# Norms of a two-block network: sums of squares with the tokens on partitions, the scale brought back by a unit-matrix product, means in column quarters

## The reference, cut to what matters

```python
def layer_norm(x, g, b):
    x32 = x.astype(jnp.float32)
    mu = jnp.mean(x32, axis=-1, keepdims=True)
    var = jnp.mean(jnp.square(x32 - mu), axis=-1, keepdims=True)
    return ((x32 - mu) * lax.rsqrt(var + LN_EPS) * g + b).astype(x.dtype)
...
        h = rmsnorm(x, norm_ffn_g[layer])
        x = x + swiglu_ffn(h, ffn_w_gate[layer], ffn_w_up[layer], ffn_w_down[layer])
    return rmsnorm(x, final_g)
...
        x = layer_norm(alpha * x + g1 * ax, ln1_g[i], ln1_b[i])
        fx = sqrelu_mlp(x * (1.0 + sc2) + sh2, mlp_w1[i], mlp_w2[i])
        x = layer_norm(alpha * x + g2 * fx, ln2_g[i], ln2_b[i])
```

## Time and profile before

| | |
|---|---|
| median of 3 runs | 3063.86 us (3062.43 to 3078.8) |
| the profiled execution | 3063.69 us |
| its span, first to last instruction | 3061.9 us, so 1.8 us lie around it |
| PE busy | 2767.5 us, 90% of the span |
| PEld, DVE, POOL, ACT busy | 71%, 45%, 44%, 23% |
| mean granted TensorE clock | 0.958 of full speed |
| DMA | 236.37 MB, 77 GB/s |

### The profile page before, as it was taken

How to read it: one execution, slowest core, us unless ns; L and a number is a source line. 1 busy time by engine, 2 the same in 40 slices (tenths; PEclk the granted TensorE clock), 3 DMA queues, 4 the chain that set the end, 5 groups by cost and what they waited for, 6 DMA issues and landing times.

```text
span 3061.9 us, 38477 instructions
## 1 busy us (share of the span) xinstructions
PE 2767.5 (90%) x13722; PEld 2174.0 (71%) x13722; DVE 1378.1 (45%) x1901; ACT 695.2 (23%) x1284; POOL 1345.4 (44%) x822
## 2 busy tenths in 40 slices
PE   7599999978999989889989999999778888899997
PEld 5366777756777768555668888888567667678885
DVE  6964222264222254444344433444675555354544
ACT  2022000012000022555321000100355455111102
POOL 6215556544555553122337443343262222486661
PEclk9799999989999999899999999999989998999999
DMA  4014444423444431000011111111101000122321
GB/s 176 28 49 138 150 147 141 148 86 119 144 137 144 143 111 63 21 1 0 14 42 62 55 62 62 61 55 62 35 28 41 27 33 22 58 89 94 96 96 48
DMA packets 66443, 236.37 MB, mean 77 GB/s; under 512 B 7104, under 2 KB 8512, under 8 KB 66112
## 3 DMA queue, kind: packets, MB, share of 16 engines
q1 hardware_dynamic: 65792, 233.64, 23.1%
q10 hardware_dynamic: 576, 1.70, 0.2%
HBM read 233.22 MB, written 2.10 MB: 77 GB/s over the span
## 4 chain that ended last, share of the span: by engine, by line
PE 76%; DVE 12%; issue 7%; ACT 3%; POOL 2%; DVEq 1%; DMA 0%; ACTq 0%; POOLq 0%; SPq 0%
PE ps L458 59%; PE ps L737 3%; PE ps L492 2%; PE ps L839 2%; PE ps L589 1%; PE ps L811 1%; PE ps L723 1%; PE ps L861 1%; DVE X L1664 1%; PE ps L507 1%; DVE rstd L1278 1%; POOL X L435 1%; DVE hlo L1654 1%; DVE arena L1369 1%; PE ps L708 1%
## 5 line engine op out<-in xcount | busy, mean ns | idle before, releaser
L369 POOL TENSOR_SCALAR whi<-raw 128x1024 fp32r<-128x1024 f32 x334 | 374.2, 1120 | 1343.9 <-DMA raw<-in_stream 1343.6
L458 PE MATMUL ps<-Ahi,whi 128*128 128x512 f32 (+1 forms) x2208 | 770.8, 379 | 132.6 <-DVE Alo L1305 41.5
L371 POOL TENSOR_TENSOR wlo<-raw,whi 128x1024 fp32r<-128x1024 f32 x334 | 823.9, 2467 | 27.9
L458 PE MATMUL ps<-Alo,whi 128*128 128x512 f32 (+1 forms) x2208 | 762.3, 375 | 0.0
L458 PE MATMUL ps<-Ahi,wlo 128*128 128x512 f32 (+1 forms) x2208 | 759.3, 374 | 0.0
L458 PEld LDWEIGHTS ps<-Ahi,whi 128*128 128x128 f32 x2208 | 396.4, 193 | 236.5 <-issue 63.9
L458 PEld LDWEIGHTS ps<-Ahi,wlo 128*128 128x128 f32 x2208 | 396.4, 193 | 74.9
L458 PEld LDWEIGHTS ps<-Alo,whi 128*128 128x128 f32 x2208 | 397.3, 193 | 70.4
L458 PE MATMUL ps<-hhi,whi 128*128 128x512 f32 x1120 | 377.0, 374 | 21.5 <-DVE X L1664 21.5
L458 PE MATMUL ps<-hhi,wlo 128*128 128x512 f32 x1120 | 372.8, 370 | 0.0
L458 PE MATMUL ps<-hlo,whi 128*128 128x512 f32 x1120 | 372.5, 370 | 0.0
(11 more groups left out here) (193 smaller groups left out, 2901.6 us busy)
## 6 DMA issues: line engine op xcount, KB each, us to landing
raw<-in_stream SPq DMA_DIRECT2D x430, 512.0 KB, 3.7
X<-in_xT SPq DMA_DIRECT2D x2, 1024.0 KB, 6.4
arena<-in_dft SPq DMA_DIRECT2D x1, 2048.0 KB, 17.3
out_xT<-X SPq DMA_DIRECT2D x2, 1024.0 KB, 4.3
X<-in_ctxT SPq DMA_DIRECT2D x1, 1024.0 KB, 18.5
arena<-in_icnt ACTq DMA_DIRECT2D x1, 1024.0 KB, 6.6
vec<-in_vec SPq DMA_DIRECT2D x1, 364.5 KB, 7.8
arena<-in_fmap SPq DMA_DIRECT2D x1, 256.0 KB, 12.8
```

What stands on the lines that cost most here:

```text
L369: pool.tensor_scalar(whi[:, s, part], raw[:, s, part], 1.0, 1.0, ALU.mult, ALU.mult).then_inc(sem("w_hi"), 1)
L371: pool.tensor_tensor(wlo[:, s, part], raw[:, s, part], whi[:, s, part], ALU.subtract).then_inc(sem("w_split"), 1)
L458: mm = pe.matmul(dst[c], w[:, b % RING, off:off + P], rhs(k, part, c0, n), start=(k == 0 and w is whi and part == 0), stop=(k == kn - 1 an ...
```

## The change

All nine norms take the form of the norm over heads. For each of the 8 tiles PE does 4 products (6 in l1 and l2) with 128x128 squares as stationary operand and one moving column of ones, where it did one or two products with 512 or 256 moving columns. ACT takes the root of 128x4 or 128x6 into the small tile sm, DVE the reciprocal of it (signal `inv`), and PE brings it back with 4 or 6 products against the unit matrix `ident`, 128 columns each, into PSUM (`norm_scale`, signal `rstd`). DVE then reads the scale from PSUM instead of from SBUF. Since POOL cannot read PSUM, DVE copies the scale to rstd at the end of l1, l2 and l3, and POOL waits for this copy (`kept`) where it waited for the last scaled tile (`m`).

The sums for the mean are taken in parts: tiles 0 to 6 by products with 32 columns of ones into one of four quarters of the partitions, tile k into quarter k modulo 4; ACT copies the partial sums times 1/32 to std; then PE adds up tile 7 and the parts with products of the full ones. The unit matrix is loaded as the third transfer of the kernel, ahead of vec and of the first weights, where it stood behind the constants.

```diff
+PARTS = {"l1": 0, "l2": 0, "l3": 0, "l4": 0}
+MEAN = {"l1": 2, "l2": 2, "l3": 1, "l4": 1}
+SQUARES = {"n1": 6, "n2": 0, "n3": 0, "n4": 0, "n5": 0, "l1": 0, "l2": 0, "l3": 2, "l4": 2}
+RSTD = {"n1": 7, "n2": 5, "n3": 7, "n4": 5, "n5": 3, "l1": 4, "l2": 4, "l3": 4, "l4": 3}
+EARLY = KT - 1
...
+        def norm_scale(name, c0, n):
+
+            return psf[:, RSTD[name] * 512 + c0:RSTD[name] * 512 + c0 + n]
+
         def keys(n):
             return [*range(*window(n)), *range(QT, NTT)]
...
                 sp.dma_start(X[:, 4 * h:4 * h + 4, 0:T], ins["xT"][:, 4 * h:4 * h + 4, :]).then_inc(sem(f"x{h}"), 16)
+            sp.dma_start(ident[:, :], ins["ident"]).then_inc(sem("unit"), 16)
             sp.dma_start(vec[:, :], ins["vec"]).then_inc(sem("vec"), 16)
             for b in range(RING):
...
-                pool.wait_ge(*when(f"{name}_m", len(cols) * KT))
+                pool.wait_ge(*when(f"{name}_kept", 1))
...
-            def column_sums(name, bank, cols, src, src_ready):
-
+            def norm_squares(name, cols):
+
+
+                tokens = sum(n for _, n in cols) // P
                 for k in range(KT):
-                    pe.wait_ge(*when(src_ready, k + 1))
-                    for c, (c0, n) in enumerate(cols):
-                        mm = pe.matmul(ps[:, bank + c, 0:n], ones[:, :], src(k)[:, c0:c0 + n],
-                                       start=(k == 0), stop=(k == KT - 1))
-                    mm.then_inc(sem(name), 1)
-
-            def squares(k):
-                return tmp[:, k % 4, :]
-
-            def rms(name, bank=0):
-                column_sums(f"{name}_sum", bank, X_ONLY, squares, f"{name}_sq")
-
-            def layernorm(name, cols, x_ready, x_before, bank=0):
-
-                for k in range(KT):
+                    pe.wait_ge(*when(f"{name}_sq", k + 1))
+                    for t in range(tokens):
+                        mm = pe.matmul(ps[:, SQUARES[name], t:t + 1], tmp[:, k % 4, t * P:(t + 1) * P], ones[:, 0:1],
+                                       start=(k == 0 and t == 0), stop=(k == KT - 1 and t == tokens - 1),
+                                       skip_group_check=True)
+                    mm.then_inc(sem(f"{name}_sum"), 1)
+                pe.wait_ge(*when(f"{name}_inv", 1))
+                for t in range(tokens):
+                    mm = pe.matmul(norm_scale(name, t * P, P), sm[:, 1, t:t + 1].to_broadcast([P, P]), ident[:, :],
+                                   start=True, stop=True, skip_group_check=True)
+                mm.then_inc(sem(f"{name}_rstd"), 1)
+
+            def layernorm(name, cols, x_ready, x_before):
+
+                for k in range(EARLY):
                     pe.wait_ge(*when(x_ready, x_before + k + 1))
                     for c, (c0, n) in enumerate(cols):
-                        mm = pe.matmul(ps[:, bank + c, 0:n], ones[:, :], X[:, k, c0:c0 + n],
-                                       start=(k == 0), stop=(k == KT - 1))
+                        q = 32 * (k % 4)
+                        mm = pe.matmul(ps[q:q + 32, PARTS[name] + c, 0:n], ones[:, 0:32], X[:, k, c0:c0 + n],
+                                       start=(k < 4), stop=(k + 4 >= EARLY), skip_group_check=True)
+                mm.then_inc(sem(f"{name}_part"), 1)
+                pe.wait_ge(*when(x_ready, x_before + KT))
+                for c, (c0, n) in enumerate(cols):
+                    pe.matmul(ps[:, MEAN[name] + c, 0:n], ones[:, :], X[:, KT - 1, c0:c0 + n], start=True, stop=False,
+                              skip_group_check=True)
+                pe.wait_ge(*when(f"{name}_parts", 1))
+                for c, (c0, n) in enumerate(cols):
+                    mm = pe.matmul(ps[:, MEAN[name] + c, 0:n], ones[:, :], std[:, c0:c0 + n], start=False, stop=True,
+                                   skip_group_check=True)
                 mm.then_inc(sem(f"{name}_mu"), 1)
-                column_sums(f"{name}_sum", bank + 2, cols, squares, f"{name}_sq")
+                norm_squares(name, cols)
 
...
 
-            def norm_std(name, bank, cols, eps):
+            def norm_std(name, tokens, eps):
                 act.wait_ge(*when(f"{name}_sum", KT))
-                for c, (c0, n) in enumerate(cols):
-                    act.activation(std[:, c0:c0 + n], ps[:, bank + c, 0:n], ACT.Sqrt, scale=1.0 / D,
-                                   bias=epsr[:, eps:eps + 1]).then_inc(sem(f"{name}_std"), 1)
+                act.activation(sm[:, 0, 0:tokens], ps[:, SQUARES[name], 0:tokens], ACT.Sqrt, scale=1.0 / D,
+                               bias=epsr[:, eps:eps + 1]).then_inc(sem(f"{name}_std"), 1)
 
...
 
-            def layernorm(name, cols, bank, use):
+            def layernorm(name, cols, use):
                 width = sum(n for _, n in cols)
+                act.wait_ge(*when(f"{name}_part", 1))
+                copy(std[:, 0:width], psf[:, PARTS[name] * 512:PARTS[name] * 512 + width], 1.0 / 32).then_inc(sem(f"{name}_parts"), 1)
                 norm_squares(name, X, f"{name}_d", 0, len(cols), width)
-                norm_std(name, bank, cols, 1)
...
 
-            def norm_rstd(name, n_std, width):
-                dve.wait_ge(*when(f"{name}_std", n_std))
-                dve.reciprocal(rstd[:, 0:width], std[:, 0:width]).then_inc(sem(f"{name}_rstd"), 1)
+            def norm_rstd(name, tokens):
+                dve.wait_ge(*when(f"{name}_std", 1))
+                dve.reciprocal(sm[:, 1, 0:tokens], sm[:, 0, 0:tokens]).then_inc(sem(f"{name}_inv"), 1)
                 dve.wait_ge(*when(f"{name}_rstd", 1))
 
             def scaled(name, k, g, dst, width=T):
 
                 return dve.scalar_tensor_tensor(out=dst, in0=X[:, k, 0:width], scalar=v(g[0], g[1] + k),
-                                                in1=rstd[:, 0:width], op0=ALU.mult, op1=ALU.mult)
+                                                in1=norm_scale(name, 0, width), op0=ALU.mult, op1=ALU.mult)
 
             def rms(name, g):
...
 
-            def layernorm(name, cols, bank, use):
+            def layernorm(name, cols, use):
 
                 width = sum(n for _, n in cols)
                 dve.wait_ge(*when(f"{name}_mu", 1))
                 for k in range(KT):
                     for c, (c0, n) in enumerate(cols):
-                        dve.scalar_tensor_tensor(out=X[:, k, c0:c0 + n], in0=ps[:, bank + c, 0:n], scalar=-1.0 / D,
+                        dve.scalar_tensor_tensor(out=X[:, k, c0:c0 + n], in0=ps[:, MEAN[name] + c, 0:n], scalar=-1.0 / D,
                                                  in1=X[:, k, c0:c0 + n], op0=ALU.mult, op1=ALU.add).then_inc(sem(f"{name}_d"), 1)
                 dve.wait_ge(*when(f"{name}_d", len(cols) * KT))
-                norm_rstd(name, len(cols), width)
+                norm_rstd(name, width // P)
                 if use is not None:
                     for nth, part in enumerate(PASSES[name]):
...
                                 split_lo_modulated(name, nth, k - 2, use, cols)
+                    dve.tensor_copy(rstd[:, 0:width], norm_scale(name, 0, width)).then_inc(sem(f"{name}_kept"), 1)
                     return
```

More of the change, by code:

```diff
@@ L151, in build @@
         share("sum", tiles)
-        share("std", {n: 2 if n in with_ctx else 1 for n in norms})
+        share("std", {n: 1 for n in norms})
+        share("inv", {n: 1 for n in norms})
         share("rstd", {n: 1 for n in norms})
+        share("part", {n: 1 for n in norms[5:]})
+        share("parts", {n: 1 for n in norms[5:]})
+        share("kept", {n: 1 for n in norms[5:8]})
         share("y", {n: KT for n in norms if n not in ("n3", "n5")})
@@ L529, in _ @@
             pe.wait_ge(*when("setup", 1))
-            rms("n1")
-            pe.wait_ge(*when("n1_std", 1))
+            pe.wait_ge(*when("unit", 16))
+            norm_squares("n1", X_ONLY)
             win = [(SPLITS[B_WIN + i], B_WIN + i) for i in range(6)]
@@ L653, in swiglu @@
                 down(i, b + 2, i % 3, 0)
-            rms("n2")
+            norm_squares("n2", X_ONLY)
             pe.wait_ge(*when("csil", 2))
@@ L658, in _ @@
             swiglu(0, "ff0", "n2_out")
-            rms("n3")
+            norm_squares("n3", X_ONLY)
             for g in range(4):
@@ L923, in normed, with rms @@
                 return tmp[:, k % 4, 0:T]
-            def rms(name, bank, ready, before, split=True):
+            def rms(name, ready, before, split=True):
                 norm_squares(name, X, ready, before, 1, T)
-                norm_std(name, bank, X_ONLY, 0)
+                norm_std(name, QT, 0)
                 if split:
@@ L956, in _ @@
             act.wait_ge(*when("setup", 4))
-            rms("n1", 0, "x", 0)
+            rms("n1", "x", 0)
             act.wait_ge(*when("lam", 2))
@@ L1044, in swiglu @@
                 rows(B0 + 4 + 5 * (FF_IT - 1), 1)
-            rms("n2", 0, "wout_evac", 0)
+            rms("n2", "wout_evac", 0)
             act.dma_start(icnt.rearrange("p a b -> p (a b)"), ins["icnt"]).then_inc(sem("icnt"), 16)
```

(22 more changed lines are left out.)

23 lines of the change are left out of this document (11 added, 12 removed).

## The result

| | before | after |
|---|---|---|
| median | 3068.26 us (20 runs, 3058.73 to 3078.8) | 3085.12 us (20 runs, 3073.35 to 3095.16) |
| profiled execution, its span | 3063.69, 3061.9 | 3087.79, 3086.0 |
| PE's mean granted clock | 0.958 | 0.944 |

The ratio is 1.0059 with a 95% interval of 1.0047 to 1.0070: slower by 16.9 us of medians. The forecast was +12.2 us, 3076, and a time within 0.5% as the likeliest class (0.57); it came out just beyond that bound, on the side that had 0.28. A second measurement in another group of runs gave 1.0067 (1.0043 to 1.0091); its profiled execution has a span of 3075.9. The two profiled executions of one kernel are 10 us apart, and the 20 runs of it 22 us: no single trace carries a difference of a few us.

The account below looks back on a forecast made before the run. PE bounds the kernel (76% of the chain of waits, DVE 12%), dense products with norms as breaks. Terms 0 + 4.7 + 1.7 + 4.5 - 1.0 + 1.7 + 0.6 + 0.4 - 0.4 = +12.2 on 3063.69 give 3076 us; range 3042 to 3096.

Parts of the forecast that it names:

- The one-column squares draw the clock down: In the norms' squares: clock falls to 0.50 about 3.7 us behind the last wide product; n2 +3.1, l1 +8.2 us.
- The rival of a clock that stays up: One-column products behind dense ones hold the clock, so squares cost what they did; -32.6, 3031 us; chance 0.13.
- The load of 128 columns at 0.107 us whatever the clock: Squares' weight loads: the skill's 107 ns names no clock; the slow clock would then add nothing to the squares.
- Root, reciprocal, way back 2.7 us for 4.1: Behind n2's squares: small root, reciprocal, hops and way back take 2.7 us where 4.1 stood before, -1.4.
- n2 and n4, +4.7 and +4.5: Slower squares and later modulation blocks delay POOL's load and the up block: +4.7 at n2, +4.5 at n4.
- The upper bound of +7.5: Upper bound for n2 and n4 each: earliest fall of the clock and a cold start of the dense run.
- n1, 0: At n1 the scale comes 3.7 late, but the long run starts where it was: 0, bounds -1 and +3.7.
- The means: Sums of X in the layer norms: 5.3 for 10.33 us at l1 and l2, -3.3 at l3 and l4.
- the rival in which they don't: Column quarters in the layer norms' sums run fully serial: +21.7, 3098 us; chance 0.08.
- Late loads that stay hidden: Rival at n2 and n4: the late load isn't waited for, 4.7 and 4.5 become 1.7 each, 3070 us; chance 0.10.
- POOL's residual waits for the copy: At l1 POOL waits for DVE's last subtraction and the copy, 0.97 plus 0.1 us; l1 +1.7 in all.
- the rows of n5 and of l2 with the heads: Stretch terms: -6.0 for n5, first mixing stage and l1's means; +2.3 for l2 from its squares, heads, l3's means.

Follow-up runs that it names:

- the change of one size: Changed kernel with all 128 columns of ones moving in the products that sum the squares, instead of one; 3033.82 us, 0.9919 of before.
- wide_filler: Changed kernel with 128 moving columns in the squares, plus 20 unread products in n2 and n4 before the up block's split; 3037.96 us, 0.9890 of before.
- kept_early: Changed kernel with DVE's copy of the scale in l1, l2 and l3 ahead of the last two splits instead of behind; 3082.53 us, 1.0063 of before.

## Why it came out so, step by step

- **The one-column squares draw the clock down.** Right, and shown by the change of one size. Forecast 10.0 at n2, 18.8 at l1 and l2, 11.4 at l3 and l4; measured 10.03 and 10.02, 18.49 to 18.90, 10.45 to 12.95. n3 and n4 had the 10.0 of n2 and took 8.91 and 11.60, 11.38 and 10.80: the point of the fall, 3.7 us behind the last wide product, is right as a middle and not for a single norm, as its two ends said. The rival of a clock that stays up is out; the rule of the Trainium skill, "TensorE: Matmul & The Clock Gate", section "What's actually happening", that PE busy-ness releases the throttle doesn't describe this trace if it is read by the profile's busy share, since 5.00 busy us of 5.00 stand beside a clock of 0.50.
- **The load of 128 columns at 0.107 us whatever the clock** (the Trainium skill, "TensorE: Matmul & The Clock Gate", section "LDWEIGHTS (loading the stationary operand)"): 25 records in 5 us at 0.50 and 48 at 1.00 are 0.200 and 0.104. Here the page's figure holds at the full clock alone.
- **Root, reciprocal, way back 2.7 us for 4.1.** Right: 241.66 to 244.29 is 2.6.
- **n2 and n4, +4.7 and +4.5.** This is the step that was mis-sized. The late load was right to 0.5 us (ready forecast for 250.9; 253.9, of which 2.5 came from n1), and so was PE's wait. But I gave the run behind it "0.5 for a rest of slow clock", and it began cold: 90 products in 23.28 us for the 20.8 plus 0.5 forecast. At n4 they took 23.55 and 22.31. wide_filler shows what the idle time costs behind wide squares, 2.9 and 1.4 us. The upper bound of +7.5 had it, as "a cold start of the dense run"; the first execution, with +7.9 and +8.4, lies beyond even that.
- **n1, 0.** Wrong by 2.5. The squares took 13.8 (forecast 13.7), and DVE, reading PSUM, no longer waited for POOL, as forecast: its scaling took 0.74 where before it took 1.52 beside POOL's splits. But the forecast had the first low part at about 27, and the third tile's products where they had begun, at 34.81. The chain shows them later:

```profile
1.79 7.38 DMA ident<-in_ident
...
9.27 13.80 PE ps L508 x64
...
27.18 2.68 DVE Alo L1301
```

The unit matrix, moved ahead in SP's queue, is now what the first product waits for: its load lands at 9.17, and the squares start 1.1 us later than before. The prediction counted the moved load nowhere. The first subtraction, with both operands in SBUF, then takes 2.68 us beside POOL's split, where the same one takes 0.68 behind POOL's work. So the low part is ready at 29.86, the first product starts at 29.90 and still at the slow pace, and the run ends at 53.28 for 50.78. (The clock column can't be used here: it reads 1.00 from the start, while 64 records take the 13.8 us of half clock.)
- **The means.** 5.53 us at l1 and l2 (forecast 5.3), 3.77 at l3 and l4 (3.6). The 28 records of the parts take 2.74, tile 7 takes 1.49 and the parts' product 1.30. The quarters overlap, and the rival in which they don't is out.
- **Late loads that stay hidden**: out, PE waits 5 us for POOL's low half in n2.
- **POOL's residual waits for the copy.** Right, in price and reason. POOL starts 18.7 us later in the trace than before and DVE's first scaled tile 14.7, so the last splits and the copy hold POOL's start up by 4.0. But its first two multiplications then take 3.65 us instead of 6.59, as DVE's splits no longer stand beside them. Against that tile the residual is complete 1.0 us later, and the forecast gave it 1.1. kept_early shows the other side of it: POOL's earlier start is paid for by DVE.

So the account is 12.2 as forecast, 2.5 for n1, and 4.2 for the cold runs at n2 and n4 less the 1.0 already in the forecast: 17.9 us, worked out, beside 16.9 of medians. That it comes so close is partly luck: it leaves out the rows of n5 and of l2 with the heads, which missed by -2.7 and +3.2 us in one execution and by -3.3 and +0.9 in the other. That the first profiled execution shows 24.1 and the second 14.0 is no step of the change, since the same kernel did both.

## What to carry to other kernels

A product with one moving column looks as cheap as its weight load and as busy as any, but here a row of them ran TensorE down to half clock, and what followed started cold. Where the load sets the pace, moving as many columns as pass in its time costs next to nothing (64 records in 7.31 us with 128 columns, 7.25 with 64, both at 1.00), and the clock stayed up or came back: here that turned +0.6% into -0.8 to -1.0%. Read the granted clock of a stretch beside its busy share before you call a form of work equal to another, and follow a moved step to its queue: with the unit matrix ahead, POOL's first split of the weights started at 12.07 us for 11.17.

## What the runs showed of the hardware that was not expected

- With 16 moving columns the clock fell as with one. With 64 it held in six norms of the eight in one execution, and where it was down (n1, l1) it did not come back within the squares. With 128 it fell at l1 or l2 in four of five traces (12.61 us instead of 10.99) and came back while the squares ran. PE was fully busy in all of these.
- DVE's splits, all operands in SBUF, took 0.54 us each alone and 1.43 beside POOL's multiplications (six in 3.25 and 8.58).
- Executions of one program differ by 22 us (3073.35 to 3095.16 in 20 runs of the changed kernel). The stretch of the heads alone took from 463 to 480 us in the three kernels with wide squares that are the same there, and 350 us of it stood at a granted clock of 0.94 in kept_early and 0.89 in wide_filler.
